# A hybrid decoder step on one core: the input in four even transfers, C transposed from two transfers, and the first gate moved up

## The reference

```python
# layer 0, mixer A
xn = _rmsnorm(h, g_mix)                                  # mean square over 1024
bu = einsum('nlgc,gpc->nlgp', xn in 64 groups of 16, bb)    # complex, from b, lam, dt
h_ = associative_scan(a, bu)                             # complex state, 64 per group
y  = einsum('nlgp,gcp->nlgc', h_re, c_re) - einsum('nlgp,gcp->nlgc', h_im, c_im) + d * xn
z  = gelu(y)
gl = z @ w_glu + b_glu                                   # 1024 x 2048
h  = h + gl[..., :1024] * sigmoid(gl[..., 1024:])
# then a convolutional FFN, a gated per-layer input, shared K/V, and layer 1 with window attention
```

## Time and profile before

| | us |
|---|---|
| median of three runs | 1419.99 (1419.76 to 1420.94) |
| the profiled execution | 1419.51 |
| its span in the trace | 1417.7 |
| PE busy | 1333.3 (94%) |
| DVE, ACT, POOL busy | 733.9, 444.8, 784.7 |

### The profile page before, as it was taken

How to read it: one execution, slowest core, us unless ns; L and a number is a source line. 1 busy time by engine, 2 the same in 40 slices (tenths; PEclk the granted TensorE clock), 3 DMA queues, 4 the chain that set the end, 5 groups by cost and what they waited for, 6 DMA issues and landing times.

```text
span 1417.7 us, 28729 instructions
## 1 busy us (share of the span) xinstructions
PE 1333.3 (94%) x10956; PEld 1293.5 (91%) x10956; DVE 733.9 (52%) x1276; ACT 444.8 (31%) x951; POOL 784.7 (55%) x699
## 2 busy tenths in 40 slices
PE   2569899999999999999999987999999999999998
PEld 2558799999999999999999954999999999999998
DVE  7788533455555551233768766555555555212254
ACT  2744211234343322101242276224333333110021
POOL 3880456555555665555655455445666655555552
PEclk9989999999999999999999999999999999999999
DMA  5034433233322233223553220322223333332322
GB/s 110 4 74 105 96 88 87 75 89 89 89 86 83 85 104 91 85 85 107 112 128 96 60 83 1 99 77 85 83 85 88 89 89 100 89 88 86 93 90 67
DMA packets 228951, 121.18 MB, mean 85 GB/s; under 512 B 25245, under 2 KB 227824, under 8 KB 228508
## 3 DMA queue, kind: packets, MB, share of 16 engines
q1 hardware_dynamic: 217688, 107.78, 26.9%
q10 hardware_dynamic: 11196, 12.46, 4.1%
HBM read 115.18 MB, written 7.07 MB: 86 GB/s over the span
## 4 chain that ended last, share of the span: by engine, by line
PE 84%; DVE 6%; ACT 5%; ACTq 2%; issue 2%; POOL 0%; DMA 0%; SPq 0%; DVEq 0%; POOLq 0%
PE ACC L879 57%; PE MI L879 10%; PE SS L879 9%; PE MI L708 3%; ACTq L1327 1%; ACT PB L1749 1%; PE SS L1215 1%; DVE T L2023 1%; DVE RSTD L2093 1%; ACT XN L1279 1%; DVE PB L2308 1%; PE SS L1093 1%; DVE T L2017 1%; ACT PTR L1279 0%; PE ACC L1030 0%
## 5 line engine op out<-in xcount | busy, mean ns | idle before, releaser
L655 POOL TENSOR_TENSOR SPL<-RAW,SPL 128x1024 fp32r<-128x1024 f32 (+2 forms) x172 | 450.0, 2616 | 14.3
L879 PE MATMUL ACC<-NH,SPL 128*128 128x272 f32 x2016 | 344.4, 289 | 0.7 <-DVE AL L2154 0.7
L652 POOL TENSOR_TENSOR TIC<-EPSB 128x1 f32<-128x1 f32 x172 | 37.0, 215 | 534.7 <-PE ACC L879 342.7
L879 PEld LDWEIGHTS ACC<-NH,SPL 128*128 128x128 f32 x2016 | 286.9, 188 | 1.8 <-issue 0.9
L879 PE MATMUL ACC<-AH,SPL 128*128 128x272 f32 x1408 | 237.5, 289 | 0.0
L879 PE MATMUL ACC<-NL,SPL 128*128 128x272 f32 x1008 | 207.9, 288 | 0.0
L879 PEld LDWEIGHTS ACC<-AH,SPL 128*128 128x128 f32 x1408 | 198.9, 188 | 0.2
L653 POOL TENSOR_SCALAR SPL<-RAW 128x1024 fp32r<-128x1024 f32 (+2 forms) x172 | 195.7, 1138 | 0.2 <-issue 0.2
L879 PEld LDWEIGHTS ACC<-NL,SPL 128*128 128x128 f32 x1008 | 158.4, 188 | 0.0
L879 PE MATMUL ACC<-AL,SPL 128*128 128x272 f32 x704 | 145.3, 287 | 0.0
L1804 DVE SCALAR_TENSOR_TENSOR ACC<-WK,CP,ACC 128x560 f32<-128x560 f32 x88 | 70.9, 806 | 97.2 <-ACT ACC L1279 90.8
(11 more groups left out here) (350 smaller groups left out, 2004.7 us busy)
## 6 DMA issues: line engine op xcount, KB each, us to landing
RAW<-in_w_up_dram SPq DMA_DIRECT2D x88, 512.0 KB
RAW<-in_w_down_dram SPq DMA_DIRECT2D x32, 704.0 KB
RAW<-in_w_glu_dram SPq DMA_DIRECT2D x16, 512.0 KB
RAW<-in_w_ple_gate_dram SPq DMA_DIRECT2D x16, 512.0 KB
KT<-bias_rows SPq DMA_DIRECT2D x64, 64.0 KB, 2.5
RAW<-in_w_q_dram SPq DMA_DIRECT2D x16, 256.0 KB
RAW<-in_w_o_dram SPq DMA_DIRECT2D x32, 128.0 KB
RAW<-in_w_ple_in_dram SPq DMA_DIRECT2D x16, 128.0 KB
```

What stands on the lines that cost most here:

```text
L652: PIN.tensor_tensor(TIC[:], EPSB[:], EPSB[:], ALU.add)
L655: PIN.tensor_tensor(lo, RAW[:, u, 0:kt, :], hi.bitcast(F32), ALU.subtract).then_inc(sem("split_done"), 1)
L879: last = mm(out[:, h, :], SPL[:, u, w, w0 + k, :], x[:, k0 + k, HT * h:HT * h + HT], start=start and k == 0 and n == 0, stop=stop and k == ...
```

## The change

The input now comes in six transfers instead of seven. The two of the samples are issued first, and then each pair of steps is one transfer of all 64 chunks (512 KB), with a semaphore of its own. ACT's squares wait for a pair at a time. C comes as it lies in memory, 32 rows of 8 KB per part, in two transfers of SP after the third pair. `CN` lies in the room of `CA`. PE brings it to its place by 64 small products with the identity (64x32 outputs, 32 rows deep) instead of eight transposes, and both copies to `CA` stand behind one `c_made`. At the gate, a one-element sigmoid (it loads the table) stands behind the copy to `VSO`, then the sigmoid of row 0 and `high_square` of row 0, and only then the stores and the loads.

```diff
-            sp.wait_ge(sem("x_first"), 64)
-            for t in range(4):
-                for a in range(2):
-                    sp.dma_start(CS_[:, 1, t, 64 * a:64 * a + 64], ...).then_inc(sem("c_in"), 16)
+            sp.wait_ge(sem("x_pair2"), 16)
+            for r, src in enumerate((ssm_c_re, ssm_c_im)):
+                sp.dma_start(CN[:, r].rearrange("q a c s -> q (a c s)"),
+                             src[0].rearrange("(q a) c s -> q (a c s)", a=2)).then_inc(sem("c_in"), 16)
...
-            pe.wait_ge(sem("c_in"), 256)
+            pe.wait_ge(sem("c_in"), 32)
             for r in range(2):
-                for t in range(4):
-                    last = turn(ACC[:, r, P * t:P * t + P], CS_[:, r, t, :], P)
-                last.then_inc(sem("c_made"), 1)
+                for c in range(CG):
+                    for a in range(2):
+                        last = mm(ACC[64 * a:64 * a + 64, r, PAIRS * c:PAIRS * c + PAIRS], CN[:, r, a, c, :],
+                                  IDN[0:PAIRS, 0:PAIRS], start=True, stop=True, skip_group_check=True)
+            last.then_inc(sem("c_made"), 1)
...
-            for i in range(4):
-                act.dma_start(XS[NSEQ:64, 2 * i:2 * i + 2, :], chunks[0:64 - NSEQ, 2 * i:2 * i + 2, :]).then_inc(sem("x_first"), 16)
             act.dma_start(XS[0:NSEQ, 0:STEPS, :], x_sample).then_inc(sem("x_in"), 16)
             act.dma_start(XS[NU_:NC_, STEPS:CH, :], x_sample).then_inc(sem("x_in"), 16)
             act.wait_ge(sem("xz_set"), 1)
-            act.dma_start(XS[64:NU_, :, :], chunks[64 - NSEQ:64]).then_inc(sem("x_in"), 16)
-            (eight transfers of the real part of C)
+            for i in range(4):
+                act.dma_start(XS[NSEQ:NU_, 2 * i:2 * i + 2, :], chunks[:, 2 * i:2 * i + 2, :]).then_inc(sem("x_pair%d" % i), 16)
...
-            copy(CA[:, r, :, 0, :], ACC[:, r, :].rearrange("p (q c) -> p q c", c=CG), scale=1.0 - 2.0 * r)
+            copy(CA[:, r, :, 0, :], ACC[:, r, :].rearrange("p (c q) -> p q c", q=PAIRS), scale=1.0 - 2.0 * r)
```

More of the change, by code:

```diff
@@ L1323, in _ @@
             act.wait_ge(sem("xz_set"), 1)
-            act.dma_start(XS[64:NU_, :, :], chunks[64 - NSEQ:64]).then_inc(sem("x_in"), 16)
[L1325 to L1328, removed]
+            for i in range(4):
+                act.dma_start(XS[NSEQ:NU_, 2 * i:2 * i + 2, :], chunks[:, 2 * i:2 * i + 2, :]).then_inc(sem("x_pair%d" % i), 16)
             act.wait_ge(sem("g_made"), 1)
             copy(GS[:], SS[:, 1, :]).then_inc(sem("g_copied"), 1)
-            act.wait_ge(sem("x_first"), 64)
-            act.wait_ge(sem("x_in"), 48)
+            act.wait_ge(sem("x_in"), 32)
             act.wait_ge(sem("xs_zero"), 1)
             for j in range(CH):
+                if j % 2 == 0:
+                    act.wait_ge(sem("x_pair%d" % (j // 2)), 16)
                 if j >= 2:
@@ L1473, in _ @@
             copy(VSO[:].rearrange("p r h n -> p (r h n)"), MI[:, 0, :]).then_inc(sem("fs_out"), 1)
-            act.wait_ge(sem("fs_out"), 1)
-            for r, (dp, ds_) in enumerate(((ssm_re_p, ssm_re_s), (ssm_im_p, ssm_im_s))):
-                store(dp[0, 0].rearrange("(q a) s -> q (a s)", a=2), FSO[:, r, :])
-                for h in range(2):
-                    store(ds_[0, 4 * h:4 * h + 4].rearrange("b (q a) s -> (b q) (a s)", a=2), VSO[:, r, h, :])
             def load_ffn(l):
@@ L1485, in load_ffn @@
                 act.dma_start(PST[0:32, 4, :], p_sample[l].rearrange("b t d -> (b t) d")).then_inc(c, 16)
-            act.wait_ge(sem("fs_ready"), 1)
-            load_ffn(0)
-            act.dma_start(RB[0:NBUCK, :], rel_bias).then_inc(sem("rb_dma"), 16)
-            act.dma_start(OHB[:], consts[0:NBUCK + 1, C_OH:C_OH + BW]).then_inc(sem("rb_dma"), 16)
+            nc.scalar.activation(TIC2[:], EPSB[:], ACT.Sigmoid)
             def gate(i):
@@ L1503, in _ @@
             high_square("n1", 0, V_GFFN, NH, True)
+            act.wait_ge(sem("fs_out"), 1)
+            for r, (dp, ds_) in enumerate(((ssm_re_p, ssm_re_s), (ssm_im_p, ssm_im_s))):
+                store(dp[0, 0].rearrange("(q a) s -> q (a s)", a=2), FSO[:, r, :])
+                for h in range(2):
+                    store(ds_[0, 4 * h:4 * h + 4].rearrange("b (q a) s -> (b q) (a s)", a=2), VSO[:, r, h, :])
+            act.wait_ge(sem("fs_ready"), 1)
+            load_ffn(0)
+            act.dma_start(RB[0:NBUCK, :], rel_bias).then_inc(sem("rb_dma"), 16)
+            act.dma_start(OHB[:], consts[0:NBUCK + 1, C_OH:C_OH + BW]).then_inc(sem("rb_dma"), 16)
             gate(1)
```

13 lines of the change are left out of this document (6 added, 7 removed).

## The result

The changed kernel takes **1415.76 us** (median; 1413.73 to 1419.06), the kernel before 1419.88 us beside it (1419.44 to 1420.94): a ratio of 0.9966, with a 95% interval from 0.9956 to 0.9977, so 4.1 us are gained. The forecast was 10.8 us. The direction was right, and 1415.76 lies just inside the range, but the forecast was 2.6 times what came.

The account below looks back on a forecast made before the run. The prediction took PE's chain of waits as the bound, with gains only in the first 50 us and at the first gate. 9.8 us at the start plus 1.0 at the gate made 10.8, median 1409.2 us, range 1405.0 to 1416.0.

Parts of the forecast that it names:

- What bounds the kernel: PE's chain of waits: edits help only where PE waits, the first 50 us and the first gate's idle 2.45 us.
- Part 1: Start, x's arrival: fourth pair at 21.0 us, squares and root end at about 25, hidden if C is later.
- Part 2: Start, C: CN lands at 22.5, clock rises during C's 6.7 us, CA starts at 29.3, 7.5 us earlier.
- Rival 1: Clock does not rise in C: C takes 7.7 us, CA at 30.3, no gain in part 3; 1412.5 us, chance 0.20.
- Part 3: x's stage at the higher clock: 2.4 and 0.8 us less, ACT waits 0.9 for POOL's BD, 9.8 us left.
- rival 2: POOL eats the lead, DVE's first scan being slow beside it: only 7.5 and 1.0 us left; 1411.5 us, chance 0.10.
- Part 4: First gate: idle 2.45 us go, transfers are 8.4 us later, PE waits 1.4 for OHB; 1.0 us gained.
- The sum: Whole kernel: 9.8 us at the start plus 1.0 at the gate, 10.8 us gained, median 1409.2 us.
- The range: Whole kernel: 1405.0 to 1416.0 us, leaving out rival 3 (C's records at 117 ns, 1421.6 us), most of rival 4, part of rival 5.
- the gate's lower end: First gate: worst end of its gain, given as 2.4 to -0.8 us around 1.0.
- Rival 4: C's records at 75 to 100 ns, or CN landing 2 us late: 1415 to 1418 us, chance 0.10.
- rival 5: C cheaper, halves overlap fully and clock rises at once: C takes 4 us; 1405.5 us, chance 0.08.

Follow-up runs that it names:

- experiment 4: Changed kernel plus 14 full 128x128 products of IDN with IDN on PE ahead of C: 1412.95 us.
- experiment 12: Changed kernel with RB and OHB issued first, first-strip pause filled, 24 full products ahead of C, and x's 64 transposes made as products with IDN: 1426.5 us.
- experiment 9: Changed kernel run once more, unedited: 1415.09 us, ratio 0.995 to the kernel before.
- experiment 2: Kernel before with only the first gate's order changed, x and C as before: 1424.1 us, ratio 1.0025.
- experiment 16: Changed kernel run a third time, unedited: 1416.4 us, ratio 0.9964 to the kernel before.
- Experiment 15: Kernel of experiment 5 plus 20 products of IDN with IDN in PE's longest pause, ahead of the first product with HSV: 1408.52 us.
- experiment 1: Kernel before with only the start changed (x and C), the first gate's order as before: 1414.98 us, ratio 0.9964.
- experiment 5: Changed kernel with RB and OHB issued first, plus 7 products of IDN with IDN in PE's pause ahead of the first strip: 1408.4 us.
- experiment 10: Kernel of experiment 5 run once more, beside the changed kernel: 1409.37 us, ratio 0.9918 to the kernel before.
- experiment 13: Changed kernel plus 13 products of IDN with IDN in PE's wait for OHB, transfers as late as before: 1413.01 us.
- experiment 7: Changed kernel with RB and OHB issued first and CN issued after x's second pair instead of its third: 1410.81 us.
- experiment 8: Kernel of experiment 7 plus 16 full products of IDN with IDN behind x's first three pairs, ahead of C: 1412.4 us.

## Why the prediction was wrong

**What bounds the kernel** held: PE's waits at the start and at the gate were the places, and all that was gained at `CA` (6.40 us) reached the first strip (145.58 for 152.12, 6.54).

**Part 1** held: pairs at 13.9, 16.3, 18.7 and 21.0 (21.0 was forecast for the last), the root at 24.9 (25), hidden behind C.

**Part 2** failed at one step: "So I expect it to rise while C is turned." `CN` was there at 23.28 (22.5 forecast: the third pair landed 0.7 later), and the 128 records took 55 ns each at one and the same clock, 7.04 us (60 ns and 7.7 at the lower level, by the row of `inputs`). Rival 1 said 30.3 for `CA`, and it was 30.37. The argument was that real products raise the clock and transposes don't. In the changed kernel 7.04 us of C's products without a pause did not raise it, experiment 4 showed it falling in the midst of them, and experiment 12 showed 27 us of dense products, 80 columns each, at the lower level. So it was not enough that the instruction was a real product.

The rise at 75.3 us, within 1.5 us of the first products, did not carry over even to the same products: in experiment 9 they ran 6.2 us at the lower level. What did raise the clock ahead of C were products of 128x128 weights and 128 columns, in experiment 4 within 22 records and 4.1 us. Depth, width and columns were not varied one by one, so which of them counts is open. The Trainium skill (TensorE: Matmul & The Clock Gate, Part 4: PE-mode transpose) says that the higher clock does not come in for transposes. The trace agrees: x's 64 transposes behind C ran at 1.07 us for eight to the last, as before. The step from there to small products was the prediction's own.

**Part 3** hung on the same step, so its 3.2 us fell with it: x's eighths stayed at 1.07 us, the wait at 1.99. Without that lead POOL's `BD` was not waited for (it came 6.38 us earlier, as ACT did), and rival 2 never arose: DVE's scan took the same 4.96 us.

**Part 4** was right in mechanism, and wrong in two terms. PE's need was forecast well: 179.1 less the 5.0 us by which PE was ahead behind the first strip is 174.1, and 173.85 came. `OHB` landed 1.9 us later than forecast. `PST` was issued 1.5 us earlier than forecast in this frame, but its transfer took 9.1 us, longer than both rows I had bounded it with (8.3 and 5.9) and 2.1 more than the 7.0 between them that I took, and `OHB` came 1.3 us behind it. The 180.5 of the sum is 173.5 + 7.0, the landing of `PST`; the 0.4 for `OHB` had been left out of it. The reason given was "The weight load is mostly over by then". It was not: of the two queues SP's, which carries the weights (q1), moved as much as ACT's (q10) from 173 to 177.5 us:

```profile
q10 hardware_dynamic: 580, 0.51, 59.9%
q1 hardware_dynamic: 975, 0.50, 48.4%
```

So the wait was 3.56 instead of 1.4. The term that was missing is the clock behind a wait: 1.4 to 3.1 us more in five traces (the changed kernel in its three executions, the gate alone, and experiment 4). Together the gate is not +1.0 but 2.45 - 3.56 - 1.5 = -2.6 in this execution, and -3.4 by experiment 2.

**The sum** with these terms: 6.4 - 2.6 = 3.8 us gained. 4.1 came (7.1 and 5.1 by the ratios of experiments 9 and 16). What the forecast had too much is thus 3.4 us for the clock at C and x (9.8 less 6.4) and 3.6 for the gate, 7.0, against the 6.7 that were missing. That it closes to 0.3 us is in part luck: it leaves out the 1.5 us of the first strip, which were lost in two of the three profiled executions of this kernel, and all low stretches behind 186 us.

The range held the time, but not for its reasons: the gate's lower end was -0.8, and what came was below it. Rival 4 named 1415 to 1418, but for C's records at 75 to 100 ns or `CN` 2 us late, and they took 55 ns, with `CN` 0.8 us late. Its chances were also added wrongly: forecast, rivals 1, 2, 5 and nine tenths of rival 4 are 0.95, not 0.91. What is left over between the executions of one kernel, 3 to 5 us, is low stretches that fall out differently each time, after 95 us, in the first strip, at 245 us and in the attention; what decides them is open. Experiment 15 did not settle it.

## What to carry to other kernels

When an instruction that may wait is moved ahead of DMA issues on the same queue, each of them becomes as late as what it waits for; put the transfers in front of it, or at least the one small transfer that the bounding engine needs next (here 4.5 us of a change worth 9). Allow for the clock behind a new pause of PE beside its length: 1.4 to 3.1 us here behind each of five waits of 2.3 to 3.7 us, 1.5 behind one of 1.9 us in 6 of 13 executions, and behind the sigmoid's pause nothing in the kernel before (2.45 us) and 1.4 us in experiment 1 (2.56 us). And don't bank on a higher clock for small products: look for rows of the same size, not only of the same kind, and for more than one of them.

## What the runs showed of the hardware

- Products with weights 32 deep and 64 wide and 32 columns take 24 ns a record at 2.4 GHz and 55 at 1.2 (experiment 4). 128 of them in a row left the clock low where it was low, and where it was up it fell during them (why is open).
- f32 products with weights 80 deep and 128 wide and 80 columns take 213 ns a record at 1.2 GHz and two records each. A transpose of the same tile takes one record of 133 ns, so a product takes 3.2 times the time (experiment 12). 27 us of them, PE busy throughout, did not raise the clock.
- Idle products of 128 columns in PE's pauses paid: 1.83 us of them ahead of the first strip (likely, by five of five executions against seven of 13) and 3.06 us in the wait for `OHB` (once, against five of five unfilled waits) left the clock up behind the pause (experiments 5, 10, 13).
- `CN` (two transfers of 256 KB), issued while two 512 KB transfers were on their way, landed 1 us later than when it was issued 2.8 us later, with one on its way (experiments 7 and 8).
